# Scale and bias of the last LayerNorm: one row each, spread over the partitions by TensorE between the last down pieces

## What is computed

```
def layer_norm(x, g, b):
    mu = jnp.mean(xf, axis=-1, keepdims=True)
    var = jnp.mean(jnp.square(xf - mu), axis=-1, keepdims=True)
    return ((xf - mu) * lax.rsqrt(var + LN_EPS)).astype(x.dtype) * g + b
...
for e in range(N_EXPERTS):
    out = out + combine[..., e:e + 1] * swiglu(x, we_gate[e], we_up[e], we_down[e])
...
x = layer_norm(ALPHA * x + ffn, ln2_g[i], ln2_b[i])
```

## Time and profile before

| | us |
|---|---|
| median of 3 runs | 1256.97 (1256.9 to 1257.2) |
| the profiled execution's own time | 1257.12 |
| its span, first to last instruction | 1255.4 |

### The profile page before, as it was taken

One profiled execution on the slowest core, in us unless ns is written; L12 is line 12 of the kernel. 1 busy time (PEld: TensorE's weight loads), 2 busy tenths in 40 slices (PEclk: granted clock), 3 DMA queues, 4 the chain that ended last, 5 costly groups with the idle time before them and its releaser, 6 DMA issues.

```text
span 1255.4 us, 15006 instructions
## 1 busy us (share of the span) xinstructions
PE 1214.8 (97%) x6061; PEld 853.4 (68%) x6061; DVE 720.1 (57%) x649; ACT 585.7 (47%) x496; POOL 39.9 (3%) x60
## 2 busy tenths in 40 slices
PE   9999999999999999999999999999999999999994
PEld 8988888888988557656755665674575566567541
DVE  6978655568888455545635643654564365455524
ACT  5576444445767245334533533543452354345321
POOL 0100000002000000000000000000000000000010
PEclk9999999999999999999999999999999999999998
DMA  9957565546458899999999999999999999999995
GB/s 317 350 173 240 196 201 184 187 134 236 151 191 323 336 404 420 404 411 420 420 420 407 419 419 419 419 420 420 406 419 419 420 420 413 421 420 417 419 395 232
DMA packets 109678, 434.43 MB, mean 346 GB/s; under 512 B 8884, under 2 KB 50916, under 8 KB 96292
## 3 DMA queue, kind: packets, MB, share of 16 engines
q1 hardware_dynamic: 106016, 421.07, 85.3%
q0 software_dynamic: 3504, 12.32, 2.7%
q10 hardware_dynamic: 84, 0.02, 0.0%
HBM read 428.40 MB, written 4.98 MB: 345 GB/s over the span
## 4 chain that ended last, share of the span: by engine, by line
PE 86%; DVE 6%; DMA 3%; ACT 3%; issue 2%; SPq 0%; DVEq 0%; ACTq 0%
PE turn L2189 16%; PE turn L2153 15%; PE turn L2193 8%; PE accp L2129 6%; PE accp L2167 6%; PE turn L1857 4%; PE turn L1854 4%; PE accp L2172 4%; DVE w_lo L1111 4%; PE accp L1745 3%; PE accp L1746 3%; PE accp L1747 3%; DMA raw<-in_we_down 3%; PE turn L1856 2%; PE turn L1855 2%; ACT w_hi L773 2%
## 5 line engine op out<-in xcount | busy, mean ns | idle before, releaser
L1111 DVE TENSOR_TENSOR w_lo<-raw,w_hi 128x2048 fp32r<-128x2048 f32 (+3 forms) x202 | 425.5, 2120 | 212.4 <-ACT w_hi L773 210.3
L773 ACT CAST w_hi<-raw 128x2048 fp32r<-128x2048 f32 (+1 forms) x196 | 352.1, 1804 | 163.6 <-DMA raw<-in_we_down 49.9
L2153 PE MATMUL turn<-raw,x_few 128*64 128x448 f32 x784 | 161.6, 547 | 2.1 <-issue 1.2
L2189 PE MATMUL turn<-w_hi,a_hi 128*128 128x448 f32 x496 | 128.5, 378 | 2.6 <-ACT y_work L956 1.1
L2189 PEld LDWEIGHTS turn<-w_hi,a_hi 128*128 128x128 f32 x496 | 87.9, 188 | 51.9 <-issue 37.2
L2193 PE MATMUL turn<-w_lo,a_hi 128*128 128x448 f32 x496 | 121.4, 367 | 0.7 <-DVE w_lo L1111 0.7
L2167 PE MATMUL accp<-w_hi,t_both 128*128 128x512 f32 x448 | 117.6, 404 | 3.6 <-ACT w_hi L773 3.6
L2189 PE MATMUL turn<-w_hi,a_lo 128*128 128x448 f32 x496 | 120.7, 365 | 0.0
L2167 PEld LDWEIGHTS accp<-w_hi,t_both 128*128 128x128 f32 x448 | 79.8, 188 | 50.9 <-issue 36.4
L2153 PEld LDWEIGHTS turn<-raw,x_few 128*64 128x64 f32 x784 | 51.1, 136 | 83.3 <-issue 75.7
L2193 PEld LDWEIGHTS turn<-w_lo,a_hi 128*128 128x128 f32 x496 | 92.5, 188 | 10.0 <-DVE w_lo L1111 2.2
(11 more groups left out here) (283 smaller groups left out, 1454.9 us busy)
## 6 DMA issues: line engine op xcount, KB each, us to landing
raw<-in_we_gate SPq DMA_DIRECT2D x97, 896.0 KB, 10.9
raw<-in_we_up SPq DMA_DIRECT2D x97, 896.0 KB, 10.2
raw<-in_we_down SPq DMA_DIRECT2D x77, 1024.0 KB, 11.0
raw<-in_w_in SPq DMA_DIRECT2D x18, 1024.0 KB, 8.6
ln_rows<-in_we_gate SPq DMA_DIRECT2D x16, 896.0 KB, 10.2
raw_more<-in_we_up SPq DMA_DIRECT2D x16, 896.0 KB, 9.6
raw_more<-in_we_down SPq DMA_DIRECT2D x14, 1024.0 KB, 11.1
raw_more<-in_we_gate SPq DMA_DIRECT2D x15, 896.0 KB, 11.0
```

The source lines that it names most:

```text
L773: nc.scalar.copy(w_hi[:, part_of(p), 0:filled(p)], raw_of(p)).then_inc(hi_done, 1)
L1111: return nc.vector.tensor_tensor(out, whole, hi.bitcast(f32), ALU.subtract)
L2153: last = nc.tensor.matmul(half_banks[which][rows, c, :], x_few[:, e % 2, k, :], w[:, h, c, :], start=(k == 0), stop=(k == KD - 1))
L2189: nc.tensor.matmul(wide_banks[:, c, :], left, wh[:, c, :], start=(k == 0 and left is x_hi_k), stop=False)
```

## The change

POOL's two loads bring the scale and the bias row to partition 0 only. Behind down piece 1 TensorE waits for both, and spreads the scale row over all partitions: a matmul with one row of ones as the stationary operand, one for each half of the row, into the banks `turn[:, 0:2]`. Behind down piece 3 it does the same with the bias row into `turn[:, 2:4]`. ACT copies each pair of banks back to `ln_rows`. DVE's last LayerNorm waits for these copies in place of the loads, and so does `last_scatter`, which writes the same banks. `bias_spread` gets the name `spread`, since the semaphore is now used for three events.

```diff
@@ POOL
             pool.wait_ge(piece_used, upto(LN_SLOT_LEFT))
-            reload_ln((ln2_g[1], ln2_b[1]))
+            for j, a in enumerate((ln2_g, ln2_b)):
+                pool.dma_start(ln_rows[0:1, j, :], a[1:2]).then_inc(ln_reloaded, 16)
@@ ACT, behind the last round_h
+            for j in range(2):
+                act.wait_ge(spread, j + 2)
+                nc.scalar.copy(ln_rows[:, j, :].rearrange("p (c d) -> p c d", c=2),
+                               turn[:, 2 * j:2 * j + 2, :]).then_inc(rows_copied, 1)
@@ DVE, finish_rows
-                dve.wait_ge(ln_reloaded, 32 * 3)
+                dve.wait_ge(rows_copied, 5)
@@ TensorE
+            def spread_ln(j):
+
+                if j == 0:
+                    pe.wait_ge(ln_reloaded, 32 * 3)
+                    pe.wait_ge(e_h, halves_before(N_UNITS))
+                for c in range(2):
+                    last = nc.tensor.matmul(turn[:, 2 * j + c, :], ones[0:1, :].bitcast(f32),
+                                            ln_rows[0:1, j, c * BANK:(c + 1) * BANK], start=True, stop=True)
+                last.then_inc(spread, 1)
+
             def last_scatter():
+
+                pe.wait_ge(rows_copied, 5)
...
             for pair in range(DOWNS[ORDER[-1]]):
                 down(N_UNITS - 1, pair)
+                if pair in (1, 3):
+                    spread_ln(pair // 2)
             last_scatter()
```

More of the change, by code:

```diff
@@ L439, in hybrid_trunk_kernel @@
         centred_ready, rows_copied_dve = sem("centred_ready"), sem("rows_copied_dve")
-        router_consts, consts_rounded, bias_summed, bias_spread, bias_ready, pos_kept = (
-            sem(n) for n in ("router_consts", "consts_rounded", "bias_summed", "bias_spread", "bias_ready", "pos_kept"))
+        router_consts, consts_rounded, bias_summed, spread, bias_ready, pos_kept = (
+            sem(n) for n in ("router_consts", "consts_rounded", "bias_summed", "spread", "bias_ready", "pos_kept"))
         silu_ready, h_whole, h_hi_ready, h_ready = (sem(n) for n in ("silu_ready", "h_whole", "h_hi_ready", "h_ready"))
@@ L1402, in _ @@
                         if j == 0:
-                            dve.wait_ge(bias_spread, 1)
+                            dve.wait_ge(spread, 1)
                             nc.vector.tensor_copy(router_bias, accp[:, 3, 0:E]).then_inc(bias_ready, 1)
@@ L2017, in _ @@
                             nc.tensor.matmul(accp[:, 3, 0:E], ones[:].bitcast(f32), bias_part, start=True,
-                                             stop=True).then_inc(bias_spread, 1)
+                                             stop=True).then_inc(spread, 1)
                     if j == 1:
```

## The result

The changed kernel takes 1267.43 us (median of 6, 1266.6 to 1269.61) against 1257.13 for the kernel before in the same comparison (median of 6): ratio 1.0083, 95% interval 1.007 to 1.0096. It is 10.3 us slower. The prediction said 7.0, with a range up to 1266.3: right in its sign and in where the time goes, too small above all in its term for the clock, and the time lies 1.1 us above the range.

What follows compares the result with a forecast made beforehand. DMA bytes were taken to bound the last 36 us. End of piece 7: 1234.6 + 8.5 + 3.4 + 1.9 + 0.4 = 1248.8, 7.0 us later than 1241.8, so 1256.97 + 7.0 = 1264.0, range 1261.2 to 1266.3.

Steps and rivals of the forecast that it cites:

- The bound: In the last 36 us: DMA bytes bind, and the end of the last down piece moves the kernel's end by as much.
- The rows late by the queue: POOL's two 4 KB loads wait behind four gathers; PE idles 8.8 us after down piece 1, until 1234.6.
- The landing: The two rows land at 1234.5, 0.6 us behind the fourth gather (1233.9); TensorE starts at 1234.6.
- whole packets drained at a time: In POOL's queue: engines draining whole packets shrink the two turns to one or none, the sum by up to 0.6 us.
- The work behind the wait: PE after the wait: 8.5 us for pieces 2 to 7, 3.4 spreading, 0.4 last record; 12.3 at full clock.
- the row of full-width float32: Profile row of eight 128-column float32 matmuls; from it 0.425 us per 512-column record, 3.4 us for four spreading matmuls.
- The cheap spreading: Rival at the spreading: one-row matmuls take 0.9 us in place of 3.4; 4.5 us later, 1261.5; chance 0.1.
- The clock: PE after the idle stretch: half speed for 3.9 us, a loss of 1.9 us.
- my long case: Rival after PE resumes: clock stays low longer, 3.9 us lost in place of 1.9; 9.0 us later, 1266.0; chance 0.13.
- The range: Whole kernel: 1261.2 to 1266.3, to hold 8 in 10; takes in the cheap spreading and my long case.
- The rival of early landing: Rival at the two small loads: they land before 1225.8, ahead of the gathers; 2.5 us faster, 1254.5; chance 0.08.

Runs made afterwards that it cites:

- the three streams: Changed kernel with the first spreading done five times over behind its wait, one, 128 or 64 rows deep: 1280.12, 1272.68 and 1281.4 us, one execution each.
- the filled wait: Changed kernel with 38 float32 matmuls of 128 columns between down piece 1 and the wait for the two rows: 1264.79 us.
- the late spreadings: Changed kernel with the two spreadings behind down pieces 5 and 6 in place of 1 and 3: 1259.59 us, ratio 1.0015.
- without the copies: Changed kernel with POOL's two loads ahead of the gathers and without ACT's two copies: 1255.43 us, ratio 0.9985.
- loads first: Changed kernel with POOL's two 4 KB loads issued ahead of the four gathers: 1255.5 us, ratio 0.9986.

## Why the prediction was too small, point by point

- **The bound** was right: the last piece's end moved from 1241.79 to 1253.16, and 13.5 us come behind it, as before (13.6). The 11.4 us between the two ends are 10.5 when each is set against the start of its down pieces.
- **The rows late by the queue** was right, and shown by moving the loads. That they cost so much because pieces 2 to 7 stand behind the wait was shown by moving the spreadings. The Trainium skill (DMA: Bandwidth & Descriptors, Queues, rings and completion order) has it that each engine consumes a queue's descriptors in ring order. The trace agrees: 14.4 and 15.1 us for 4 KB behind the gathers. (The prediction puts the signals of all 16 engines under that section too; they stand in the same page's section Why a DMA increments its semaphore by 16 and not by 1.)
- **The landing** was forecast 0.6 us behind the fourth gather; it was 1.0. Set against the start of the down pieces, PE resumed 12.7 us later (1235.98 - 1223.24), where the forecast has 12.2: 0.5 us. In the second trace of the changed kernel it is 13.3 us. A landing sooner than forecast, by whole packets drained at a time, did not come.
- **The work behind the wait** was 12.8 us for 12.3: 0.5 us. That the row of full-width float32 stands for a matmul one row deep was right: 1.9 us for two of them, where the plain sum is 1.7. At half speed two take 3.70 us from start to start for a sum of 3.4, and ten take 17.36 for 17.0: the excess is about the same for two and for ten, so it goes with the changes of mode at both ends and not with each matmul. The cheap spreading is ruled out.
- **The clock is the step that failed.** I put down 1.9 us, "at half speed for 3.9 us", from the one return of the clock in the trace of before. There PE had resumed with down pieces, two side by side over all 128 rows. Here it resumed with one-row matmuls, which the runs show not to bring the clock back: 3.8 us at half speed for them, 5.2 for the down pieces behind. The loss is 4.4 us, 2.5 more than forecast. Even my long case, 3.9, fell short. The depth is not all of it: with spreadings 128 rows deep the clock came back 5.9 us after PE resumed, still 2.0 more than I took. The row I took it from was of a shorter idle stretch: 2.66 us, with the clock still at 1.00 as PE resumed at 1231.29 and low only from 1231.8. Here it had been low for 4.7 us when PE resumed. Whether that is what makes up the 2.0 stays open.
- **The sum** of the three, 0.5 + 0.5 + 2.5 on the forecast 7.0, is 10.5, against 10.3 measured. That they meet so closely is in part luck: the sum is read from one trace, and the second gives 1.1 + 0.5 + 2.2 on 7.0, or 10.8.
- **The range** was too narrow above. It ended at the long low clock, to which I had given 0.13, with nearly nothing added for a miss of the other terms; and all three terms erred the same way.
- **The rival of early landing** didn't happen. Its price, 2.5 us, was tried apart: 2.1.

## What to carry to other kernels

A load that has become tiny still waits its turn behind what its queue has been given: ask where it stands in the queue before asking how many bytes it has, and issue it ahead of the gathers if its slot is free by then. A wait put into the middle of TensorE's order holds all pieces behind it, landed or not. And after a long idle stretch, look at what PE resumes with: here PE stayed at half speed through the shallow matmuls and until full-depth ones had run for 3 to 5 us. Making the spreadings deep gained 1.0 us at most; not having the idle stretch gained 11.9. The version that beats both kernels is the changed one with POOL's two loads ahead of the gathers, 1255.5 us, about 2 us under the kernel before (ratio 0.9986).

## What the runs showed of the hardware

- The granted clock did not return during 17.3 us of unbroken matmuls 1 or 64 rows deep, and did return 5.0 us into the same stream 128 rows deep. The Trainium skill (TensorE: Matmul & The Clock Gate, Part 1: The HAM clock gate) calls the warm-up a budget of time and not of a number of matmuls. By that, the three streams would be alike; the deep one's execution is 7 to 9 us shorter than the other two, and the measurement decides. Each of the three streams was seen in one execution.
- The clock can also drop around 1222, at the start of the down pieces, for 3.3 us. It did so in 5 of the 14 traces (from 1222.4 with the filled wait, from 1223.1 with the late spreadings, also in the 128-row and 64-row streams and without the copies) and not in others (before, both of the changed kernel, loads first), though PE's work ahead is the same. PE is busy 3.44 of the 5.40 us from 1217.0 to 1222.4 both in the kernel before and with the filled wait. Such a drop costs the down pieces some 1.6 us (5.28 in place of 3.65 us for pieces 0 and 1 with the filled wait) and is part of how single executions differ. What decides it stays open.
